# Second attention: groups of four units with two-head value products, in place of a pipeline of pairs

## The reference, cut to what matters

```python
o_c, o_s, o_w = nsa_attention(q_n, kc, vc, ks, vs, kw, vw)   # compressed, selected, window
g = jax.nn.sigmoid(g_b)...
o_n = g[..., 0:1] * o_c + g[..., 1:2] * o_s + g[..., 2:3] * o_w
y_b = from_heads(o_n...) @ w_o_nsa
mixed = jax.nn.sigmoid(gate_a) * y_a + jax.nn.sigmoid(gate_b) * y_b     # y_a: the first attention
x = x + mixed @ w_out
```

## Time and profile before

| what | value |
|---|---|
| median of 3 runs | 2299.63 us (2294.74 to 2300.18) |
| the profiled execution's own time | 2294.53 us |
| its span, first to last instruction | 2292.7 us |
| PE busy | 2243.6 us, 98% |
| weight loads busy | 1792.0 us, 78% |
| POOL / DVE / ACT busy | 65% / 50% / 27% |
| the chain that ended last | PE 92%, DVE 4% |
| mean granted TensorE clock | 0.994 |

### The profile page before, as it was taken

How to read it: one execution, slowest core, us unless ns; L and a number is a source line. 1 busy time by engine, 2 the same in 40 slices (tenths; PEclk the granted TensorE clock), 3 DMA queues, 4 the chain that set the end, 5 groups by cost and what they waited for, 6 DMA issues and landing times.

```text
span 2292.7 us, 31066 instructions
## 1 busy us (share of the span) xinstructions
PE 2243.6 (98%) x11648; PEld 1792.0 (78%) x11648; DVE 1143.1 (50%) x1800; ACT 614.5 (27%) x1440; POOL 1489.3 (65%) x679
## 2 busy tenths in 40 slices
PE   8999999999999999999999999999999999999998
PEld 6876888888877767778888888877677788888886
DVE  7868577772362275557540243542555576421422
ACT  5248222220020155531220121111355512200200
POOL 7650787778864704448887888764324377887884
PEclk9999999999999999999999999999999999999999
DMA  5220233223322301112223232332111122222322
GB/s 191 102 74 2 74 102 101 95 99 101 110 86 93 126 10 56 47 56 96 92 98 101 93 101 93 101 101 89 59 38 47 56 83 83 101 101 92 101 92 74
DMA packets 54925, 195.77 MB, mean 85 GB/s; under 512 B 7312, under 2 KB 7312, under 8 KB 54544
## 3 DMA queue, kind: packets, MB, share of 16 engines
q1 hardware_dynamic: 52496, 187.85, 24.2%
q10 hardware_dynamic: 2304, 6.12, 0.7%
HBM read 191.72 MB, written 2.10 MB: 85 GB/s over the span
## 4 chain that ended last, share of the span: by engine, by line
PE 92%; DVE 4%; DMA 1%; issue 1%; POOL 1%; ACT 0%; SPq 0%; DVEq 0%; POOLq 0%
PE bank L471 26%; PE bank L473 25%; PE bank L472 25%; PE bank L575 4%; PE bank L609 4%; PE bank L586 3%; DMA w_raw<-wstream 1%; PE bank L547 1%; PE bank L487 1%; PE bank L508 1%; PE bank L639 1%; DVE cols L1281 1%; POOL w_lo L419 1%; PE bank L538 0%; POOL w_hi L416 0%
## 5 line engine op out<-in xcount | busy, mean ns | idle before, releaser
L416 POOL TENSOR_TENSOR w_hi<-w_raw,zero 128x1024 fp32r<-128x1024 f32 x336 | 645.0, 1920 | 751.3 <-PE bank L473 667.5
L419 POOL TENSOR_TENSOR w_lo<-w_raw,w_hi 128x1024 fp32r<-128x1024 f32 x336 | 845.2, 2515 | 26.3
L471 PE MATMUL bank<-hn_hi,w_hi 128*128 128x512 f32 x1632 | 653.0, 400 | 13.9 <-POOL w_lo L419 12.6
L473 PE MATMUL bank<-hn_hi,w_lo 128*128 128x512 f32 x1632 | 638.9, 391 | 0.0
L472 PE MATMUL bank<-hn_lo,w_hi 128*128 128x512 f32 x1632 | 638.3, 391 | 0.0
L471 PEld LDWEIGHTS bank<-hn_hi,w_hi 128*128 128x128 f32 x1632 | 308.2, 189 | 79.8 <-POOL w_lo L419 9.8
L473 PEld LDWEIGHTS bank<-hn_hi,w_lo 128*128 128x128 f32 x1632 | 307.8, 189 | 65.9
L472 PEld LDWEIGHTS bank<-hn_lo,w_hi 128*128 128x128 f32 x1632 | 308.4, 189 | 62.7 <-issue 2.2
L471 PE MATMUL bank<-hid_hi,w_hi 128*128 128x512 f32 x688 | 267.6, 389 | 0.0
L472 PE MATMUL bank<-hid_lo,w_hi 128*128 128x512 f32 x688 | 267.6, 389 | 0.0
L473 PE MATMUL bank<-hid_hi,w_lo 128*128 128x512 f32 x688 | 267.6, 389 | 0.0
(11 more groups left out here) (285 smaller groups left out, 2727.5 us busy)
## 6 DMA issues: line engine op xcount, KB each, us to landing
w_raw<-wstream SPq DMA_DIRECT2D x352, 512.0 KB, 3.6
x<-xT SPq DMA_DIRECT2D x4, 512.0 KB, 7.8
out<-yout ACTq DMA_DIRECT2D x8, 256.0 KB, 2.2
mem_x<-memT SPq DMA_DIRECT2D x1, 1024.0 KB, 12.4
lnc<-lncount ACTq DMA_DIRECT2D x1, 1024.0 KB, 5.6
cs<-trig ACTq DMA_DIRECT2D x2, 512.0 KB, 3.3
par<-params ACTq DMA_DIRECT2D x1, 696.0 KB, 5.2
fc<-fconst ACTq DMA_DIRECT2D x1, 592.0 KB, 6.9
```

The lines of the kernel that those rows point to most:

```text
L416: nc.gpsimd.tensor_tensor(w_hi[:, slot, :], w_raw[:, slot, :], zeros, ALU.add).then_inc(w_rounded, 1)
L419: nc.gpsimd.tensor_tensor(w_lo[:, slot, :], w_raw[:, slot, :], w_hi[:, slot, :].bitcast(f32), ALU.subtract).then_inc(w_split, 1)
L471: nc.tensor.matmul(ps[bank][:, 0:cols_], wh, a_h, start=c == 0, stop=False)
L473: mm = nc.tensor.matmul(ps[bank][:, 0:cols_], wl, a_h, start=False, stop=c == chunks - 1)
```

## The change

The units of the second attention are ordered so that four that follow one another are the same kind and tile for two heads of each key group. Every engine's `attend` runs the fox part and the first group as before in pairs, with scores and masks ahead of the turnings in the gated steps, and then 16 iterations over groups of four. PE's iteration g: scores of the next group's four units, its four masks, turnings of this group's four units, half a gate linear, `group_values` of this group, the other half of the linear. `group_values` multiplies one value chunk by two heads' probabilities at once (256 columns, `pT[:, r:4:2, ...]`), and the output of a group is 128x256. In the last iteration there are no scores, and the fox linears of the first two mix tiles stand before and after the values in place of a gate linear; the mix loop then leaves these two out.

```diff
-        UN = [(k, p + 4 * r, t) for p in range(4) for t in T_ORDER for k in ("sel", "win") for r in range(2)]
+        UN = [(k, p + 4 * r, t) for both in ((0, 1), (2, 3)) for t in T_ORDER for k in ("sel", "win") for p in both
+              for r in range(2)]
...
+            def group_values(j):
+                kind, h, t = units[j][:3]
+                pe.wait_ge(p_kept, j + 4)
+                if kind == "sel":
+                    pe.wait_ge(o_lo, outputs_before(j))
+                for c in range(t + 1):
+                    for r in range(2):
+                        nc.tensor.matmul(ps[6][HD * r:HD * r + HD, 0:2 * P],
+                                         vsw[:, 0 if kind == "sel" else 1, c, r * HD:(r + 1) * HD],
+                                         pT[:, r:4:2, c * P:(c + 1) * P], start=c == 0 and kind == "sel", stop=False)
                 if kind == "win":
...
+                    for n in range(2):
+                        for r in range(2):
+                            h_ = h % 4 + n
+                            mm = nc.tensor.matmul(ps[6][HD * r:HD * r + HD, n * P:(n + 1) * P],
+                                                  vbd[:, r, h_ * HD:(h_ + 1) * HD],
+                                                  cprobT[:, t, r * P:(r + 1) * P], start=False, stop=n == 1)
                     mm.then_inc(pv_done, 1)
...
+            def attend(u0, u1, freed, un=None, gate_tiles=(), mix=()):      # PE
+                for i in range(u0, u1 + 6 if un is None else un + 4, 2):
+                    gated_ = un is not None and i >= un
                     if u0 < i < u1:
...
                         scores(i, u0, freed)
+                    if gated_:
+                        causal_ends(i, 2)
+                    if u0 <= i - 4 < u1:
                         turn(i - 4, u0)
                     if i - 6 >= u0:
                         values(i - 6)
+                    if gated_:
...
+                        linear(gate_tiles[0], hn_hi, hn_lo, S, DC, part=(0, 4) if i == un else (4, 8))
+                        continue
...
+                values(un - 2)
+                for g in range(1, 17):
+                    j = un + 4 * (g - 1)
+                    if g < 16:
+                        scores(j + 4, u0, freed)
+                        scores(j + 6, u0, freed)
+                        causal_ends(j + 4, 4)
+                    turn(j, u0)
+                    turn(j + 2, u0)
+                    if g == 1:
+                        pe.wait_ge(cmp_kept, 2 * (LIN_OF[u0] + 1))
+                    if g < 16:
+                        linear(gate_tiles[g], hn_hi, hn_lo, S, DC, part=(0, 4))
+                        group_values(j)
+                        linear(gate_tiles[g], hn_hi, hn_lo, S, DC, part=(4, 8))
+                    else:
+                        pe.wait_ge(o_lo, outputs_before(un))
+                        linear(mix[0], ya_hi, ya_lo, S, 4, last=False)
+                        group_values(j)
+                        linear(mix[1], ya_hi, ya_lo, S, 4, last=False)
...
+                for g in range(1, 17):                                      # ACT
+                    j = un + 4 * (g - 1)
+                    keep_turned(j)
+                    keep_turned(j + 1)
+                    act.wait_ge(*took(gate_tiles[g - 1]))
+                    A(sg[:, g - 1, :], sg[:, g - 1, :], ACT.Tanh, scale=0.5).then_inc(gated, 1)
+                    if g < 16:
+                        exp_row(j + 4)
+                    keep_turned(j + 2)
+                    keep_turned(j + 3)
+                    if g < 16:
+                        for u in range(j + 5, j + 8):
+                            exp_row(u)
...
+                for g in range(1, 17):                                      # DVE
+                    j = un + 4 * (g - 1)
...
+                    V.tensor_tensor(sg[:, g - 1, :], ps[3][:, :], rs[:, :], ALU.mult).then_inc(dve_took, 1)
+                    if g < 16:
+                        minima(j + 4)
+                        minima(j + 6)
+                        scale_rows(j + 4)
+                    if units[j][0] == "win":
+                        write_output(j, *group_output(j), 2 * P)
+                    if g < 16:
+                        scale_rows(j + 6)
```

More of the change, by code:

```diff
@@ L359, in output, with group_output @@
                 return ya_hi[:, h // 2, cols_], ya_lo[:, h // 2, cols_]
-            return yn_hi[:, h % 4, cols_], yn_lo[:, h % 4, cols_]
+            raise AssertionError(kind)
+        def group_output(u):
+            _, h, t = units[u][:3]
+            return [y[:, h % 4:h % 4 + 2, t * P:(t + 1) * P] for y in (yn_hi, yn_lo)]
         def outputs_before(u):
-            return sum(1 for v in range(0, u, 2) if units[v][0] != "sel")
+            pairs = sum(1 for v in range(0, u, 2) if units[v][0] not in GATED)
+            return pairs + sum(1 for v in range(0, u, 4) if units[v][0] == "win")
         RUNS = [(RING, B_L + TURNS), (B_L + TURNS + 24, B_L + LAYER_BLOCKS + TURNS),
@@ L617, in values @@
-                if kind != "sel":
-                    mm.then_inc(pv_done, 1)
[L620 to L625, removed]
+                                              start=c == 0, stop=c == n - 1)
+                mm.then_inc(pv_done, 1)
+            def group_values(j):
[8 more added lines that the diff above has]
+                                         pT[:, r:4:2, c * P:(c + 1) * P], start=c == 0 and kind == "sel", stop=False)
+                if kind == "win":
+                    for n in range(2):
[4 more added lines that the diff above has]
+                                                  cprobT[:, t, r * P:(r + 1) * P], start=False, stop=n == 1)
+                    mm.then_inc(pv_done, 1)
@@ L626, in attend, with causal_ends @@
+            def causal_ends(i, n):
+                for u in range(i, i + n):
+                    t = units[u][2]
+                    nc.tensor.matmul(s_bank(u)[:, t * P:width(u)], identb, causal, start=False,
+                                     stop=True).then_inc(scored, 1)
+            def attend(u0, u1, freed, un=None, gate_tiles=(), mix=()):
+                for i in range(u0, u1 + 6 if un is None else un + 4, 2):
+                    gated_ = un is not None and i >= un
                     if u0 < i < u1:
@@ L629, in attend @@
                         scores(i, u0, freed)
[L630 removed]
+                    if gated_:
+                        causal_ends(i, 2)
+                    if u0 <= i - 4 < u1:
                         turn(i - 4, u0)
                     if i - 6 >= u0:
[L633 to L634 removed]
                         values(i - 6)
[L636 to L640, removed]
+                    if gated_:
+                        if i == un:
+                            pe.wait_ge(c_kept, TT * (LIN_OF[u0] + 1))
+                        linear(gate_tiles[0], hn_hi, hn_lo, S, DC, part=(0, 4) if i == un else (4, 8))
+                        continue
                     for n in (i, i + 1):
@@ L847, in _ @@
                 u0, u1 = FIRST["fox", l], FIRST["nsa", l] + len(UN)
-                attend(u0, u1, first_free, FIRST["nsa", l], ph["gates"])
+                attend(u0, u1, first_free, FIRST["nsa", l], ph["gates"], [pair[0] for pair in ph["mix"]])
                 for m in range(DC):
                     fox_, nsa_ = ph["mix"][m]
-                    if m == 0:
-                        pe.wait_ge(o_lo, outputs_before(u1) - 16)
-                    linear(fox_, ya_hi, ya_lo, S, 4, last=False)
+                    if m >= 2:
+                        linear(fox_, ya_hi, ya_lo, S, 4, last=False)
                     if m == 0:
@@ L947, in keep_turned, with attend @@
                 A(pT[:, u % 4, 0:width(u)], ps[4 + u % 2][:, 0:width(u)], ACT.Copy).then_inc(p_kept, 1)
-            def attend(u0, u1, gates_from=None, gate_tiles=()):
-                for i in range(u0, u1 + 4, 2):
+            def attend(u0, u1, un=None, gate_tiles=()):
+                for i in range(u0, u1 + 4 if un is None else un + 4, 2):
                     for n in (i, i + 1):
-                        if gates_from is not None and n < gates_from:
+                        if un is not None and n < un:
                             compressed(u0, n - u0)
[L954 to L957, removed]
                     for r in range(2):
@@ L1292, in scale_rows, with write_output, attend @@
                                     ALU.mult).then_inc(p_scaled, 1)
[L1294 to L1306, removed]
+            def write_output(j, hi, lo, n):
+                dve.wait_ge(pv_done, outputs_before(j) + 1)
+                src = ps[6][:, 0:n]
+                if len(hi.shape) == 3:
+                    src = src.rearrange("p (h n) -> p h n", n=P)
+                V.tensor_copy(hi, src).then_inc(o_hi, 1)
+                dve.wait_ge(o_hi, outputs_before(j) + 1)
+                V.tensor_tensor(lo, src, hi.bitcast(f32), ALU.subtract).then_inc(o_lo, 1)
```

(4 more changed lines are left out.)

39 lines of the change are left out of this document (17 added, 22 removed).

## The result

The changed kernel takes 2303.48 us (median of 12 runs, 2299.61 to 2310.82), the kernel before 2297.34 us (median of 12, 2291.70 to 2303.35). The medians differ by 6.1 us; the ratio is 1.0029, 95% interval 1.0017 to 1.0041, which is slower by 6.7 us (3.9 to 9.4). Forecast were +8.0 us and 2307.6 us.

The account below looks back on a forecast made before the run. PE, busy 98% of the span, was taken as the bound. Terms -8.1 + 0.9 - 1.0 - 0.3 - 1.4 + 17.9 = +8.0 us, added to the median 2299.63, gave 2307.6 us; forecast range 2304 to 2313.

Parts of the forecast that it names:

- The new wait: Turnings of a group: third unit waits for ACT's copy of the first, 0.56 us a group, 17.9 in all.
- Fewer fixed parts: Groups of four pay the fixed costs between PE's phases once: 0.27 us saved a group, 8.1 in 30 groups.
- turnings to linear: Joint in each group: the first linear matmul behind the turnings costs 0.08 us extra.
- Masks to turnings: Joint in each group, not in the trace: between 0 and 0.10 us, taken as 0.05.
- the two other bounded joints: Linear to scores and linear to values, not in the trace: between nothing and 0.20 us, each taken as 0.095.
- The opening: Two opening steps and lone values: +0.9 us in two layers; scores and masks fill the first turning's wait, -1.0 us.
- Wide products: Values of two heads in one product: 160 pairs of 128 columns become 80 of 256, 0.3 us saved.
- The tail: Behind the last gate linear, two fox linears around the last values: 0.7 us saved a layer, 1.4 in all.
- Waits that stay hidden: Scores waiting for scaled rows: no PE wait expected, 1.1 us of slack in the tightest case.
- the first (both effects cancel): Rival for the total: larger saving or shorter stall gives +0.5 us, from -3 to +4, about 2300; chance 0.25.
- The second (faster): Rival: joints of linears and masks cost nothing on entry, 15.3 us saved in groups, about 2293 us; chance 0.15.
- the third and fourth: Rivals: exponentials become the loop, about 2320 us, chance 0.08; two-head products lose side-by-side running, 2342 us, chance 0.02.

Follow-up runs that it names:

- e1: Changed kernel with the first chunk of the linear between a group's first two and last two turnings; 2284.75 us against 2298.63, ratio 0.9939.
- e6: Changed kernel with ACT doing the next group's first exponential ahead of the copies of the first two turned units; stretch 231.09 us a layer, +14.45.
- e3: Changed kernel with value products of one head and 128 columns again, twice as many; first layer's stretch 216.73 us against 216.64.
- e4: Changed kernel with the two fox linears around the last group's values put back in the mix loop; stretch 217.26 us, +0.62.
- e7: Kernel before, with one fox linear behind its last turning and one behind its last values; stretch 213.33 us, +0.06.
- e2: Changed kernel with the next group's scores and masks between a group's first two and last two turnings; 2287.08 us, ratio 0.9951.
- e8: Changed kernel with one linear chunk between the turnings, values behind the whole linear, and DVE's output copy an iteration later; 2279.08 us against 2299.07, ratio 0.9917.
- e5: Kernel before, with scores and masks ahead of the turnings in each gated pair step; stretch 217.36 us against 213.27.

## Why the prediction was right, step by step

The sign, the mechanism and its place were right; the net is 6.7 us where 8.0 stood. Of the 4.1 us by which the forecast of 2307.6 missed the median of 2303.48, 2.3 come from its starting point: the three runs of the kernel before had their median at 2299.63 us, the twelve at 2297.34. The gated part, to the first nsa linear and less the fox linears in it, was to grow from 168.5 to about 173 us a layer; it is 171.6 from the first turning, and 172.4 with the scores and masks that now stand ahead of that turning.

- *The new wait.* Forecast 0.56 us a group, 17.9 in all. Taking it away by e1 gives 9.2 us a layer, 0.57 a group, 18.4 in all; e6 shows ACT's copy as the releaser. That 128 and 512 columns would wait alike was forecast from the earlier trace rows and came: 0.52 in both, where 0.50 stood. Its sum at 512 columns, 0.66 + 0.585 + 0.14, is 1.385 and not 1.37, which gives 0.51. One of its signs of being wrong, an idle under 0.4 in the turnings of a group, would have misled by the column that prints idle time (0.35); the starts of rows decide.
- *Fewer fixed parts.* Forecast with the tail, the opening and the wide products: 9.9 us saved. Measured: e1, which has no wait, is 5.8 us a layer under the kernel before (213.27 - 207.44), 11.7 in all. These are the terms that were off, by 1.8 us together. The part that I took too high is turnings to linear (0.08): e1 shows it as nothing, 1.3 us a layer, which the other errors partly take back. Masks to turnings was 0.01 to 0.02, not 0.05 (four masks and their joint take 0.24). Of the two other bounded joints the chosen value of 0.095 held: ahead of scores and ahead of values a linear's last matmul takes 0.32 us instead of 0.23.
- *The opening.* Forecast: scores and masks fill the wait of 0.66 us. They do for the first turning:

```profile
852.18 0.49 PE L582 MATMUL bank<-ksw,qb 64*128 64x128 f32 x4
852.60 0.28 PE L642 MATMUL bank<-bc 128*128 128x128 bf16 x2
852.91 0.77 PE L593 MATMUL bank<-fc,prow 128*128 128x128 f32 x4
...
853.35 0.29 DVE L1351 TENSOR_TENSOR ya_lo<-bank,ya_hi 128x128 fp32r<-128x128 f32 x1
...
853.79 0.88 PE L614 MATMUL bank<-pT,va 128*64 128x128 f32 x12
```

  0.2 of wait is left at 852.91. But from the first of these four turnings to the next phase it is 0.88 us, and was 0.70 before. The turnings themselves keep their pace (the second unit's starts 0.36 us behind the first's in both kernels); the rest is a wait of the values phase. It may not start until DVE has written the previous output out of the same bank, and that write (L1351) ends at 853.64, 0.15 us ahead of the values. Before, the scores stood between the turnings and these values and hid it. The prediction did not have this wait, which is of the same kind as the new wait in the groups; it is read from the trace alone, and no run removed it. So 0.35 a layer was won, not 0.5.
- *Wide products.* Forecast 0.3 us, measured 0.3 to 0.4 (e3). The 0.213 us a pair that this term starts from stands in no row, so that the size came out right is partly luck.
- *The tail.* Forecast 0.7 a layer from moving to a group's tail and fewer joints. From the end of the last gate linear to the end of the stretch it is 49.00 us before (1010.46 to 1059.46), of which 0.43 are two pairs of value products that now stand earlier, and 48.48 after (1019.97 to 1068.45), of which 0.52 are the new wait: 0.6 saved. e4 and e7 split what the linears themselves do: 0.62 in the new order, where they hide a copy, and -0.06 in the old one. The prediction had counted joints alone and had not seen that, without the linears, the new order would add a wait of 1 us there.
- *Waits that stay hidden.* Forecast: none at the scores. None appeared, and neither in e1, e2 and e8, whose iterations are shorter.

The rivals: the first (both effects cancel) put +0.5 and at most +4, where 6.7 came. Of its two premises the larger saving nearly came (11.7 us in all against its 12.3); the shorter wait did not (18.4 against 12.8). With the cost per product that is e3's rival, the prediction's sum would be +4.3 us, inside the interval of the measured ratio (3.9 to 9.4): the total does not exclude it, e3 does. The second (faster) needed linears without joints, and e5 excludes that; the third and fourth did not occur: PE has no wait for scaled rows at scores, and the values phases became shorter (25.95 us against 29.62, of which 0.7 is the opening wait).

## What to carry to other kernels

Putting work of one kind together saves the joints between kinds, but it also puts instructions next to one another that share a buffer through another engine; what stood between them had hidden that round trip. Before grouping, write down for each pair of neighbours in the new order who must empty the buffer in between, and compare the chain (last write, other engine's pass, release) with the work that stands there now; one piece of independent work, set exactly there, kept the gain here, whether it was a chunk of a linear (e1) or the next scores (e2). More banks for the turnings would be another way; that was not tried. Where totals spread by 0.5%, compare a stretch of equal work between two landmarks in the traces: here it was reproducible to 0.1 us and gave the effect of each part.

## What the runs showed of the hardware that I had not expected

- A linear behind turnings starts its first matmul 0.07 to 0.08 us before the turnings' pitch is over, and gives it back in that matmul (0.32 instead of 0.23, e1): the sum is next to nothing. Behind values the first matmul takes 0.34 us (878.70 to 879.04 in the changed kernel) with no such early start.
- Two kernels ran the same code at different speeds outside the change. In the changed kernel's profile the granted clock was 0.70 in a window in which it was 1.00 in the kernel before. First before, then after; in both, PE had just done 16 products of one column (637.62 to 639.43 in the changed kernel) and was back in full linears:

```profile
636.00:642.00 6.00, 5.93 (x35) 4.90 (x33) 2.56 (x5) 0.26 (x1) 1.00 (x1) 1.00 0.27 90
642.00:645.00 3.00, 3.00 (x15) 2.49 (x14) 0.00 (x0) 0.00 (x0) 0.49 (x1) 1.00 0.00 0
```

```profile
636.00:642.00 6.00, 5.92 (x32) 4.79 (x31) 2.57 (x5) 0.26 (x1) 1.02 (x1) 0.89 0.30 90
642.00:645.40 3.40, 3.40 (x12) 2.72 (x11) 0.00 (x0) 0.00 (x0) 0.00 (x0) 0.70 0.00 0
```

  A value under 1.00 is a mean over time at 2.4 and at 1.2 GHz. Most of what puts the start of the stretch at 846.19 us in one profile and at 851.81 in the other are such windows. Over the whole span the mean granted clock is 0.994 of 2292.7 us before and 0.990 of 2309.0 after, by which an estimated 14 and 23 us are lost, 9 of the 16 us between the spans. The change itself accounts for 6.7. What decides whether the clock falls at such a place was not tried.
